# The first norm's root moved behind conv's products, its operand formed in one pass, the start's loads reordered, and products on zeros ahead of the first chunk

## What is computed

```python
def rms_norm(x, g):
    y = xf * lax.rsqrt(jnp.mean(xf * xf, axis=-1, keepdims=True) + EPS)
    return (y * g).astype(x.dtype)

def conformer_conv(h, w_in, dw, dw_b, ln_g, ln_b, w_out):
    a, b, z = jnp.split(h @ w_in, 3, axis=-1)
    v = a * jax.nn.sigmoid(b)
    v = depthwise_conv31(v, dw) + dw_b
    v = jax.nn.silu(layer_norm(v, ln_g, ln_b))
    return (v * jax.nn.silu(z)) @ w_out

x = x + conformer_conv(rms_norm(x, conv_norm), ...)
```

## Time and profile before

| | |
|---|---|
| time, median of 3 runs | 2292.33 us (2290.73 to 2294.69) |
| time of the profiled execution | 2295.96 us |
| its span, first to last instruction | 2294.2 us |
| TensorE busy in the span | 2251.2 us (98%) |
| VectorE, ScalarE, GpSimd busy | 1634.9, 1144.7, 244.6 us |
| TensorE busy from 0 to 50 us | 28.15 us |
| read from memory | 405.71 MB, 178 GB/s over the span |

### The profile page before, as it was taken

One profiled execution on the slowest core, in us unless ns is written; L12 is line 12 of the kernel. 1 busy time (PEld: TensorE's weight loads), 2 busy tenths in 40 slices (PEclk: granted clock), 3 DMA queues, 4 the chain that ended last, 5 costly groups with the idle time before them and its releaser, 6 DMA issues.

```text
span 2294.2 us, 35885 instructions
## 1 busy us (share of the span) xinstructions
PE 2251.2 (98%) x13708; PEld 2006.7 (87%) x13708; DVE 1634.9 (71%) x2452; ACT 1144.7 (50%) x1373; POOL 244.6 (11%) x81
## 2 busy tenths in 40 slices
PE   6999999999999999999999999999999999999999
PEld 5999988888888888888888878888888888888888
DVE  6877876778877777777777767666665566655666
ACT  5666564555555555555444555454433334333433
POOL 4888930000000000000000000000000000000000
PEclk9999999999999999999999999999999999999999
DMA  5555555444444444566444333534555555555556
GB/s 220 186 184 184 181 179 188 167 169 174 171 166 166 166 167 163 184 248 240 154 149 161 132 129 140 187 133 165 183 185 190 193 184 183 189 194 184 184 201 219
DMA packets 57429, 409.46 MB, mean 178 GB/s; under 512 B 6496, under 2 KB 6624, under 8 KB 8544
## 3 DMA queue, kind: packets, MB, share of 16 engines
q1 hardware_dynamic: 57312, 407.84, 49.6%
HBM read 405.71 MB, written 2.10 MB: 178 GB/s over the span
## 4 chain that ended last, share of the span: by engine, by line
PE 93%; DVE 3%; ACT 2%; DMA 1%; issue 1%; SPq 0%; DVEq 0%; ACTq 0%
PE G L351 25%; PE G L352 25%; PE G L353 13%; PE G L350 13%; PE G L359 4%; PE G L360 4%; PE G L361 4%; DMA RAW<-stream_dram 1%; DVE LO L335 1%; ACT HI L328 1%; PE A L1055 1%; PE A L1033 1%; PE A L1020 0%; PE A L2199 0%; PE A L1039 0%
## 5 line engine op out<-in xcount | busy, mean ns | idle before, releaser
L328 ACT ACTIVATE HI<-RAW 128x2048 fp32r<-128x2048 f32 x381 | 728.6, 1913 | 784.4 <-DMA RAW<-stream_dram 779.9
L335 DVE TENSOR_TENSOR LO<-RAW,HI 128x2048 fp32r<-128x2048 f32 x332 | 759.9, 2290 | 140.4 <-ACT HI L328 137.8
L352 PE MATMUL G<-HX,HI 128*128 128x512 f32 x1544 | 623.3, 404 | 1.7 <-DVE LO L335 1.2
L351 PE MATMUL G<-HX,HI 128*128 128x512 f32 x1544 | 612.7, 397 | 0.0
L350 PE MATMUL G<-HX,LO 128*128 128x256 f32 x1544 | 436.0, 282 | 0.0
L353 PE MATMUL G<-HX,LO 128*128 128x256 f32 x1544 | 434.5, 281 | 0.0
L351 PE MATMUL G<-HXB,HI 128*128 128x512 f32 x992 | 394.1, 397 | 0.0
L352 PE MATMUL G<-HXB,HI 128*128 128x512 f32 x992 | 391.2, 394 | 2.3 <-DVE X L671 1.7
L350 PEld LDWEIGHTS G<-HX,LO 128*128 128x128 f32 x1544 | 290.8, 188 | 67.3
L353 PEld LDWEIGHTS G<-HX,LO 128*128 128x128 f32 x1544 | 291.5, 189 | 61.0
L352 PEld LDWEIGHTS G<-HX,HI 128*128 128x128 f32 x1544 | 295.9, 192 | 5.8 <-DVE LO L335 2.8
(11 more groups left out here) (354 smaller groups left out, 2369.0 us busy)
## 6 DMA issues: line engine op xcount, KB each, us to landing
RAW<-stream_dram SPq DMA_DIRECT2D x381, 1024.0 KB, 4.8
X<-x_dram SPq DMA_DIRECT2D x4, 512.0 KB, 5.4
MB<-mem_dram SPq DMA_DIRECT2D x4, 512.0 KB, 7.3
out_dram<-X SPq DMA_DIRECT2D x4, 512.0 KB, 7.8
CON<-constants_dram SPq DMA_DIRECT2D x1, 996.0 KB, 16.7
VEC<-vectors_dram SPq DMA_DIRECT2D x1, 623.5 KB, 17.8
VEC<-vectors_dram SPq DMA_DIRECT2D x1, 272.0 KB, 7.2
CON<-constants_dram SPq DMA_DIRECT2D x1, 64.5 KB, 1.9
```

The source lines that it names most:

```text
L328: nc.scalar.activation(HI[:, c.slot(RING), :], RAW[:, c.slot(RING), :], ACT.Copy).then_inc(hi_ready, 1)
L335: nc.vector.tensor_tensor(LO[:, c.slot(RING), :], RAW[:, c.slot(RING), :], HI[:, c.slot(RING), :].bitcast(F32), ALU.subtract).then_inc(lo_ ...
L351: return nc.tensor.matmul(res, wh, both[:, k, :, :], start=False, stop=last)
L352: nc.tensor.matmul(res, wh, both[:, k, :, :], start=first, stop=False)
```

## The change

- The squares, the sum and the root no longer stand ahead of the first products. The operand is X times its gain: ScalarE writes `HH` straight from X (a copy with the gain as scale, one tile at a time), VectorE writes `HL` as X times gain minus `HH` (one `scalar_tensor_tensor` for a tile).
- The first two chunks are multiplied one after the other, without the lag.
- Squares, sums and root come behind the first chunk's result; TensorE's product by ones stands behind the second chunk.
- In conv every result of `G` is multiplied by the root on VectorE: the gate (`rooted_gate`) and z (`rooted_z`) when they are read, and the value through the sigmoid (`rooted_sigmoid`). VectorE reads all banks of `G` now (but for the first two chunks), and the reads stand between the taps of the block before (`between`). ScalarE's Sigmoid and Silu work in place in SBUF.
- SyncE issues chunk 0 first, then the gain, X, chunk 1, the ones, chunk 2, the vectors, chunk 3.
- TensorE multiplies zeros (`idle_turns`) 18 times before the first chunk, and 1, 2 and 1 times between the groups of the first chunk.

```diff
+        def idle_turns(pe, n):
+            for _ in range(n):
+                nc.tensor.matmul(A[0][:, 0:T], SQ[:, 0, 0:P], SQ[:, 1, :], start=True, stop=True)
...
+            act.preload_act_table_set("natural_log_exp_and_others")
             split_hi(act, At(0))
+            for g in range(len(START)):
+                high(g)
+            split_hi(act, At(1))
+            split_hi(act, At(2))
+            act.wait_ge(mm_done, 1)
+            r = conv_result(0, 0)
+            nc.scalar.activation(SG[:, 0, :], gres(r), ACT.Copy).then_inc(g_free[r.slot(NG)], 1)
+            square(0)
+            square(1)
+            split_hi(act, At(3))
+            square(2)
+            square(3)
+            act.wait_ge(s_vec, 32)
             n.root(act)
...
         def start_pe(pe, n):
-            pe.wait_ge(s_x[0], 48)
+            pe.wait_ge(cv_pad, 1)
+            idle_turns(pe, 18)
...
+            groups(0, (0, 1, 2, 1, 0))
+            groups(1, (0, 0, 0, 0, 0))
+            pe.wait_ge(s_vec, 32)
             pe.wait_ge(n_ss, START_ADDS)
             nc.tensor.matmul(A[n.bank][:, 0:T], ONES, LR[:], start=True, stop=True).then_inc(n_ss, KT - START_ADDS)
...
+                    ins = nc.vector.scalar_tensor_tensor(HL[:, ft, :], X[:, ft, :], vec(n.gain, ft), HH[:, ft, :].bitcast(F32),
+                                                         ALU.mult, ALU.subtract)
+                ins.then_inc(h_ready, 1)
+
+            nc.vector.memset(SQ[:], 0.0).then_inc(cv_pad, 1)
...
+            split_lo(dve, At(0))
+            dve.wait_ge(s_x[0], 32)
+            for g in range(len(START)):
...
+                low(g)
+            split_lo(dve, At(1))
             for g in range(1, KT // GRP):
                 dve.wait_ge(n_sq, GRP * (g + 1))
...
             def gate(z):
-                wait(act, mm_done, conv_chunk(z, 2) + 1)
-                r = conv_result(z, 2)
-                nc.scalar.activation(SZ[:, z, :], gres(r), ACT.Silu).then_inc(g_free[r.slot(NG)], 1)
+                taken(act, conv_result(z, 2))
+                nc.scalar.activation(SZ[:, z, :], SZ[:, z, :], ACT.Silu).then_inc(cv_gate, 1)
...
+            def rooted_z(z):
+                r = conv_result(z, 2)
+                wait(dve, mm_done, conv_chunk(z, 2) + 1)
+                nc.vector.tensor_tensor(SZ[:, z, :], gres(r), RR[:], ALU.mult).then_inc(g_free[r.slot(NG)], 1)
+
+            def between(ft):
+
+                if ft == KT - 1:
+                    return {8: lambda: rooted_z(KT - 5), 20: lambda: rooted_z(KT - 4)}
+                if ft == 0:
+                    at = (3, 7, 14)
+                elif z_after(ft) is None:
+                    at = (8, 12, 18)
+                else:
+                    at = (18, 21, 24)
+                plan = {at[0]: lambda: rooted_gate(ft + 1), at[1]: lambda: rooted_sigmoid(ft + 1), at[2]: lambda: value(ft + 1)}
+                if z_after(ft) is not None:
+                    plan[8] = lambda: rooted_z(z_after(ft))
+                return plan
...
             step("c0")
+            rooted_z(KT - 3)
             dve.wait_ge(cv_ln, 1)
...
             step("n2")
-            for f in range(KT - 6, KT - 4):
-                taken(dve, conv_result(f, 2))
+            rooted_z(KT - 2)
+            dve.wait_ge(cv_gate, KT - 4)
             behind = ["c2", "n3", "c3", "n4"]
             gated(0)
             for g in range(len(TWOS)):
...
                 low(g)
                 if g < len(behind):
                     step(behind[g])
+                if g == 2:
+                    rooted_z(KT - 1)
```

More of the change, by code:

```diff
@@ L497, in build @@
         START_ADDS = KT // GRP + 1
+        cv_root = sem("cv_root")
+        def idle_turns(pe, n):
+            for _ in range(n):
+                nc.tensor.matmul(A[0][:, 0:T], SQ[:, 0, 0:P], SQ[:, 1, :], start=True, stop=True)
         def start_act(act, n):
[L501 to L504, removed]
@@ L519, in start_act @@
[L519 to L525, removed]
-        def start_pe(pe, n):
-            pe.wait_ge(s_x[0], 48)
+                act.wait_ge(s_x[0], 32)
+                if k0 >= GRP:
+                    act.wait_ge(s_x[k0 // GRP], 16)
+                for ft in range(k0, k1):
+                    ins = nc.scalar.activation(HH[:, ft, :], X[:, ft, :], ACT.Copy, scale=vec(n.gain, ft))
@@ new lines, in start_pe, with groups @@
+        def start_pe(pe, n):
+            pe.wait_ge(cv_pad, 1)
+            idle_turns(pe, 18)
+            def groups(m, turns):
+                for g, (k0, k1) in enumerate(START):
+                    if not m:
+                        pe.wait_ge(h_ready, H_CONV + g + 1)
+                    if g == 0:
+                        pe.wait_ge(lo_ready, m + 1)
+                    for k in range(k0, k1):
+                        mm = product3(gres(conv_result(0, m)), conv_chunk(0, m), k, HX, k, k == 0, k == KT - 1)
+                    if turns[g]:
+                        idle_turns(pe, turns[g])
+                mm.then_inc(mm_done, 1)
+            groups(0, (0, 1, 2, 1, 0))
+            groups(1, (0, 0, 0, 0, 0))
+            pe.wait_ge(s_vec, 32)
@@ L548, in start_dve @@
             nc.vector.tensor_tensor(LR[:], SZ[:, 0, :], SZ[:, 1, :], ALU.add).then_inc(n_ss, 1)
[L549 to L576, removed]
+            dve.wait_ge(s_vec, 32)
         x_half = sem("x_half")
@@ L765, in first_taps @@
                 wait(act, cv_dw, ft + 1)
[L766 removed]
+                if ft:
+                    taken(act, conv_result(ft, 1))
+                else:
+                    act.wait_ge(cv_root, 3)
                 wait(act, cv_done, ft - 1)
@@ new lines, in value @@
+            def value(ft):
+                c, r = conv_chunk(ft, 1), conv_result(ft, 1)
+                dve.wait_ge(cv_root, 3 + ft)
+                wait(dve, mm_done, c + 1)
+                nc.vector.tensor_tensor(VP[:, ft % 2, PAD:PAD + T], gres(r), SG[:, ft % 2, :],
+                                        ALU.mult).then_inc(g_free[r.slot(NG)], 1)
+            def rooted_z(z):
+                r = conv_result(z, 2)
+                wait(dve, mm_done, conv_chunk(z, 2) + 1)
+                nc.vector.tensor_tensor(SZ[:, z, :], gres(r), RR[:], ALU.mult).then_inc(g_free[r.slot(NG)], 1)
@@ L924, in conv_dve @@
                     if TWOS[g + 1][0] >= KT - Z_LATE:
-                        for f in range(*TWOS[g + 1]):
-                            taken(dve, conv_result(f, 2))
+                        dve.wait_ge(cv_gate, TWOS[g + 1][1])
                     gated(g + 1)
@@ L2506, in _ @@
                 sp.dma_start(X[:, g:g + GRP, :], x_in[:, g:g + GRP, :]).then_inc(s_x[g // GRP], 16)
+            first_load(1)
+            sp.dma_start(CON[:, 0:K_FIRST], constants[:, 0:K_FIRST]).then_inc(s_vec, 16)
+            first_load(2)
             sp.dma_start(VEC[:, KT:V_FIRST], vectors[:, KT:V_FIRST]).then_inc(s_vec, 16)
-            for s in range(RING):
-                sp.dma_start(RAW[:, s, :], stream[C_CONV + CONV_ORDER[s]]).then_inc(raw_ready[s], 16)
+            first_load(3)
             sp.dma_start(CON[:, K_FIRST:], constants[:, K_FIRST:]).then_inc(s_rest, 16)
```

84 lines of the change are left out of this document (49 added, 35 removed).

## The result

The changed kernel takes 2299.1 us (median of 14 runs, 2296.03 to 2307.05); the kernel before took 2292.22 in the same set (14 runs, 2290.73 to 2295.7). The ratio is 1.0030, 95% interval 1.0022 to 1.0037: 6.9 us slower, where 2289.9 was forecast and 2295.5 was the upper end of the range.

A forecast was written before the change was run, and what follows sets the result against it. The prediction took TensorE, busy for 98% of the span, as the bound, so only its waits count. Start 10.0 gained, conv's end 4.2 and clock 1.7 + 1.7 lost: 2.4 us gained, 2289.9 us, range 2285.0 to 2295.5.

The forecast's parts named there:

- The start: Before steady work: the third chunk starts at 28.5 instead of about 38.5, 10.0 us gained (9 to 11).
- Conv: Conv's blocks: VectorE's three multiplications by the root add about 1.0 us a block, it still waits for TensorE; nothing lost.
- Rival C: Conv: VectorE holds the banks, each block costs TensorE 0.5 us, 8 us go, 5.6 slower, 2295.5 to 2298; chance 0.10.
- Conv's end: Last chunks of conv: VectorE's reads come late and TensorE waits, 4.2 us lost in all (2.0 to 5.0).
- block 15: Conv's end, chunk 45: TensorE's second sum waits for the block's square, delayed by a read among its taps; 2.0 us lost.
- chunk 49's bank: Conv's end: TensorE waits 3.3 us for the bank until VectorE has read chunk 47, done at 310.1.
- The clock: TensorE's clock: two new waits of 3.3 us probably drop the level, 1.7 us lost each (0 to 3.4).
- The zeros lift the clock: Start: products on zeros take 4.6 us at the lower level, then run at the higher; the 18 turns end at 11.5.
- rival B: Start: the zeros don't lift the clock, only 2.6 us gained there, 5.0 us slower in all, 2297.3; chance 0.08.
- The sum: Whole kernel: 10.0 - 4.2 - 1.7 - 1.7 = 2.4 us gained, a median of 2289.9, 0.1% less.

The follow-up runs named there:

- Experiment 2: Changed kernel, with one input of the squares' adds in PSUM, where ScalarE writes the first four squares: 2294.55 us, ratio 1.0009 to the kernel before.
- experiment 5: Changed kernel, with chunk 44 read behind block 15, its square ahead of the gate, chunk 47 read one step earlier: 2297.36 us, ratio 1.0021.
- experiment 1: Changed kernel, with the root for the sigmoid's multiplication read from a PSUM copy: 2297.73 us, ratio 1.0022 to the kernel before.
- the three edits: Changes to the changed kernel: sigmoid's root in PSUM (alone 2297.73 us), one input of the squares' adds in PSUM (2294.55), conv's end reordered (2297.36).
- experiment 6: Changed kernel with sigmoid's root in PSUM, squares' adds with one input in PSUM, and conv's end reordered, all together: 2286.14 us, ratio 0.9972.
- experiment 3: Changed kernel, with the low parts of chunks 2 and 3 made by VectorE ahead of the adds, not by GpSimd: 2298.25 us, ratio 1.0021.

## Why the prediction was wrong

- **The start, 10.0 us gained: 5.5 in the profile.** Up to the last square every time was right within 0.5 us (first chunk out at 18.96 for 19.3, squares at 24.94 for 25.4). The step that failed is "from the last square's end to the product by ones it was 13.77 - 11.14 = 2.6": it took 7.4. That row came from a stretch in which GpSimd stood still; the change moved the adds to where GpSimd forms low parts. Experiment 2, which changes only the adds' operands, gives 28.16 for the forecast 28.0.
- **Conv, nothing lost: 4.0 us in waits.** "The three multiplications by the root add about 1.0 us to a block" holds for two of them; `rooted_sigmoid` took 3.15 instead of 0.42 and the sum is 3.8. The prediction gave no row for it; the price that it took, 0.35 from start to start, is that of rows with one input in PSUM. Of the 4.0, 2.69 came by the chance told above. Rival C had the place (VectorE's queue holds the banks) but neither the mechanism nor the price, at a chance of 0.10; the forecast said "no TensorE wait between 60 and 270 us", and that sign went wrong at 61.38.
- **Conv's end, 4.2 lost: 3.6.** Nearly right in size: 1.92 for block 15 (forecast 2.0), 2.27 at chunk 49's bank (3.3), less the 0.59 that went. The bank's mechanism is shown by experiment 5. For block 15 the read among the taps, as forecast, gives 1.72 alone (experiment 1), but the held multiplications give 1.55 without it (experiment 5), which the forecast didn't have; that its number fits is in part luck.
- **The clock, 3.4 lost: 7.9.** Two stretches were forecast, 1.7 each, and four came: 2.8 behind the wait for the sum, 1.7 at chunk 49 as forecast, 1.7 behind the wait at 61.38, and 1.7 behind block 15's wait, which the forecast had as a wait of 2.0 but gave no clock.
- **The zeros lift the clock**: right, and rival B fell. By stretch of the changed kernel (columns as above; two records are one turn):

```profile
1.00:5.00 4.00, 3.54 (x10) 2.93 (x11) 0.48 (x3) 1.03 (x1) 0.00 (x0) 1.00 0.82 266
5.00:10.00 5.00, 5.00 (x25) 4.41 (x24) 2.43 (x2) 4.37 (x8) 0.00 (x0) 1.00 1.02 382
```

Ten records in 3.5 us, then 25 in 5.0. Up to 4.18 they start 0.43 apart, from 4.51 on 0.21: the higher level, reached on zeros alone. (The clock column is 1.00 in both and no guide here: in the kernel before it is 1.00 from 20 to 30 us too, where products of 256 columns start 0.21 apart, against 0.12 from 31 us on.) But what this was to bring was not on the path.
- **The sum.** Forecast 2.4 gained; the profiled execution is 9.9 longer (2305.83 - 2295.96). The miss of 12.3 is 4.5 at the start, 4.0 in conv, 4.5 in clock, less 0.6 at the end. The first two are the hold, and 2.8 of the clock's 4.5 stand behind their waits (1.1 at the start, 1.7 behind 61.38); the other 1.7, behind block 15, has both causes. At the medians the miss is 9.2 (2299.1 - 2289.9): the execution profiled lies 6.7 above the median of the changed kernel, its like before 3.6.

The Trainium skill (SBUF — State Buffer, SBUF: two separate sides) states the rule that I did not weigh: VectorE and GpSimd share a port pair as "an exclusive lock, not a bandwidth split", taken for a whole instruction, and a VectorE operation with two SBUF inputs needs it against a GpSimd operation that reads SBUF. The runs agree: the end of a held instruction follows GpSimd's end by 0.3 us (256 columns) or 1.1 (1024). It would also explain why the kernel before copies mean and root of its layer norm to PSUM.

What stays open: why the three edits alone do not add up to what they gain together. A part is shown: block 15's wait has two causes, each enough for it (1.72, 1.87 and 1.55 us with one of the edits, none with all), so no single edit gets it back. The clock is the likely rest, but each kernel was profiled once, and runs of the changed kernel spread over 11 us.

## What to carry to other kernels

When an instruction is moved, ask which engines work at its new place, not only what it waits for; a duration read beside an idle engine is no price beside a busy one. A VectorE operation with both inputs in SBUF is priced with GpSimd's instruction in front of it: look for groups of one form and size with different means, and put one of the inputs into PSUM. If a kernel copies a small operand to PSUM for no visible reason, find the reason before writing the next one.

## What the runs showed of the hardware

- Reach of the hold: here 0.42 became 2.3 to 4.8 us (15 instructions in conv), up to the length of GpSimd's own 4.6. The profile books it as busy time of VectorE, so no list of waits names GpSimd. It goes the other way too: one of GpSimd's low parts took 5.31 us beside the adds, where the median is 4.62.
- `scalar_tensor_tensor` taps, with `VP` in SBUF and the running sum in PSUM, kept 0.40 from start to start beside GpSimd all through conv.
- The length of a wait alone does not tell whether the clock falls. A wait of 3.58 ahead of the product by ones was followed by a low stretch in experiment 2 (mean 0.72 from 28 to 34) and by none in experiment 6. One of 1.87 for block 15's sums was followed by one in experiment 3 (granted clock 0.50 from 289 to 292), and one of 1.87 at the same place was not in experiment 2. I had taken the gaps of before for a rule; what decides is not shown.
